# Latent attention, pair by pair: values summed one pair later, both heads' weights turned in a row, Silu behind the exponentials

## The chip, the cores and the metric

The kernel runs on one core of one Trainium2 chip. The metric is the device time of one execution in microseconds (us). TensorE (PE, with its weight loads as PEld), VectorE (DVE), ScalarE (ACT), GpSimd (POOL) and SyncE (SP) each work through their own list of instructions in order and wait for each other by semaphores that only count up.

## What is computed

Two blocks are applied to one sequence of 256 tokens of width 1024. The first is a retention layer (4 heads) followed by a latent attention layer (16 heads); the second is a recurrent and attention hybrid with a feed-forward part. The change touches only the latent attention, which is

```
q = (_rms_norm(q_lat, q_norm) @ w_uq)       # 16 heads, 128 plain + 64 rotary columns each
kv = (lat @ w_up)                           # 128 key columns and 128 value columns per head
sc = (q_nope . k_nope + rope(q) . k_rope) * scale     # causal, two blocks of 128 queries
p = softmax(sc)
o = p @ v
return (o * silu(gate)) @ w_out
```

## The kernel before

Every weight matrix comes from HBM in units of up to 128x2048 numbers, four raw slots deep (`load`, issued on SP). ACT rounds a unit to its high part (`act_hi`, L1039), DVE subtracts to get the low part (`dve_lo`, L1496), and PE multiplies in three terms, high x high, high x low, low x high (`mm3`, L364 to L366). `act_hi(u)` waits until PE has finished unit u-4 (semaphore `w_used`), `dve_lo(u)` waits for `act_hi(u)`, and PE waits for `dve_lo(u)` before unit u. Both splitting steps are written three units ahead of PE (`AHEAD`).

The 16 heads go in 8 pairs. Pair `pair` uses four units: gate, two of the query, one of keys and values. On PE these give four groups of projections, and the attention of the pair before is put between them: the scores (`pe_scores`, L674 and L679) after the gate unit; the turning of head 0's softmax weights (`pe_turn_p`, L689, three transposes of 128x128) after the query units; head 1's turning and both heads' values (`pe_values`, L699 and L700) after the key and value unit. The eighth pair's attention stands between the first units of the output projection (`pe_output`, unit 0 to 5, with "hooks" called ahead of a unit; `U_BOUT` is the number of its first unit).

Around that, DVE masks the scores (`dve_masked`, L1756), ACT takes the exponentials (`act_exps`, L1189), DVE divides by the sum (`dve_normal`, L1767 and L1770, which raises `b_p`), PE turns, ACT copies the turned weights to SBUF (`act_pT`, L1198, which raises `b_pT`), PE sums the values, DVE multiplies by the gate (`dve_og`, L1779), ACT rounds (`act_oT`, L1203), POOL makes the low part (`pool_oT`, L2136). ACT also takes Silu of the gate projection (L1213), and copies queries and keys (L1223, L1231); DVE copies the values' projection (`b_v`, L1809) and makes the rotary products (L1732, L1735). Silu and Exp lie in different tables, so ACT loads a table ahead of each.

The order on each engine is written out by hand. In the output projection DVE's list is `lo(U_BOUT+3)`, `lo(U_BOUT+4)`, masked head 0, masked head 1, normal head 0, `lo(U_BOUT+5)`, normal head 1, `lo(U_BOUT+6)` and so on: head 1's weights are divided behind the splitting of unit `U_BOUT+5`, whose `act_hi` waits until PE has finished unit `U_BOUT+1`.

Of the kernel before, what the change touches and what calls it, by code (L numbers as in the profile page):

```python
# [6 lines left out]
ACT = mybir.ActivationFunctionType  # L7
# [696 lines left out]
def pe_pair(k, pair):  # L704

    T, s, ps = k.T, k.s, k.ps
    u = U_PAIR + 4 * pair
    if pair:
        T.wait_ge(s["b_gate"], pair)
    feature_major(k, u, k.xT, KD, 2 * VH, halves(ps[:, 0, :]))  # L710
    if pair == 0:
        T.wait_ge(s["b_lat"], 1)
        for n in range(2):
            pe_turn_pair(k, "lat", n, lambda t, c: k.b_lat[:, t, c * P:(c + 1) * P], ps[:, 4 + n, :])
        T.wait_ge(s["turned_lo"], TURN["qlat"] + 3)
    else:
        pe_scores(k, pair - 1)
        T.wait_ge(s["b_qn"], pair)
    for n in range(2):
        wh, wl = weights(k, u + 1 + n, 3, 2 * QC)  # L720
        for q, out in enumerate((ps[:, 1, 0:S], ps[:, 1, S:2 * S], ps[:, 2, 0:S])):
            if q == 2 and n == 0 and pair:
                T.wait_ge(s["b_turned"], pair)
            for c in range(3):
                m = mm3(k, out, tuple(z[:, c, q * P:(q + 1) * P] for z in (wh, wl)),
                        tuple(z[:, 3 * n + c, :] for z in k.b_qlatT), n == 0 and c == 0 and q != 1, n == 1 and c == 2)
                if q == 0 and c == 0 and head_signals(u + 1 + n):
                    m.then_inc(s["w_head"], 1)
        m.then_inc(s["w_used"], 1)
    if pair:  # L730
        pe_turn_p(k, pair - 1, 0)
        T.wait_ge(s["b_kn"], pair)
    else:
        T.wait_ge(s["turned_lo"], TURN["lat"] + 2)
    wh, wl = weights(k, u + 3, 4, 2 * KC)
    for h in range(2):
        for c in range(4):
            m = mm3(k, ps[:, 3, h * S:(h + 1) * S], tuple(z[:, c, h * P:(h + 1) * P] for z in (wh, wl)),
                    tuple(z[:, c, :] for z in k.b_latT), h == 0 and c == 0, c == 3)
            if h == 0 and c == 0 and head_signals(u + 3):  # L740
                m.then_inc(s["w_head"], 1)
    if pair:
        T.wait_ge(s["b_v"], pair)
    for t in range(NT):
        for c in range(4):
            m = mm3(k, ps[:, 4, t * S:(t + 1) * S], tuple(z[:, c, t * P:(t + 1) * P] for z in k.b_latT),
                    tuple(z[:, c, 2 * NOPE:2 * KC] for z in (wh, wl)), t == 0 and c == 0, c == 3)
    m.then_inc(s["w_used"], 1)
    if pair:
        pe_turn_p(k, pair - 1, 1)  # L750
        pe_values(k, pair - 1, 0)
        pe_values(k, pair - 1, 1)


def pe_attention_hooks(k):
    T, s, last = k.T, k.s, HB // 2 - 1

    def banks_read():
        T.wait_ge(s["b_gate"], last + 1)
        T.wait_ge(s["b_qn"], last + 1)  # L760

    def outputs_split():
        T.wait_ge(s["b_oT_lo"], last)

    def keys_read():
        T.wait_ge(s["b_turned"], last + 1)
        T.wait_ge(s["b_kn"], last + 1)

    def last_split():
        T.wait_ge(s["b_oT_lo"], last + 1)  # L770

    return {0: [banks_read],
            1: [lambda: pe_scores(k, last)],
            2: [lambda: pe_turn_p(k, last, 0), outputs_split],
            3: [lambda: pe_values(k, last, 0), lambda: pe_turn_p(k, last, 1), keys_read],
            4: [lambda: pe_values(k, last, 1)],
            6: [last_split]}


# [421 lines left out]
def act_oT(k, pair):  # L1201
    k.A.wait_ge(k.s["b_og"], pair + 1)
    k.A.activation(k.b_oT[0][:, 2 * pair:2 * pair + 2, :], k.b_og[:, :, :], ACT.Copy).then_inc(k.s["b_oT_hi"], 1)  # L1203


def act_pair(k, pair):
    A, s, ps, par = k.A, k.s, k.ps, pair % 2
    u = U_PAIR + 4 * pair
    act_hi(k, u + AHEAD)
    A.wait_ge(s["w_used"], u + 1)  # L1210
    if pair >= 2:
        A.wait_ge(s["b_og"], pair - 1)
    A.activation(k.b_gate[:, par, :, :], ps[:, 0, :].rearrange("p (h s) -> p h s", h=2), ACT.Silu).then_inc(s["b_gate"], 1)  # L1213
    if pair:
        act_exps(k, pair - 1, 0)
        act_exps(k, pair - 1, 1)
    else:
        for n in range(2):
            act_turned(k, "lat", n, ps[:, 4 + n, :], k.b_latT[0], k.b_kvnorm)
    act_hi(k, u + 1 + AHEAD)  # L1220
    act_hi(k, u + 2 + AHEAD)
    A.wait_ge(s["w_used"], u + 3)
    A.activation(k.b_qn[:, par, :, :], ps[:, 1, :].rearrange("p (h s) -> p h s", h=2), ACT.Copy).then_inc(s["b_qn"], 1)  # L1223
    if pair:
        act_pT(k, pair - 1, 0)
    act_hi(k, u + 3 + AHEAD)
    if pair:
        act_pT(k, pair - 1, 1)
        act_oT(k, pair - 1)
    A.wait_ge(s["w_used"], u + 4)  # L1230
    A.activation(k.b_kn[:, par, :, :], ps[:, 3, :].rearrange("p (h s) -> p h s", h=2), ACT.Copy).then_inc(s["b_kn"], 1)  # L1231


def act_attention_output(k):

    A, s, d, last = k.A, k.s, k.d, HB // 2 - 1
    act_hi(k, U_BOUT + AHEAD)
    act_hi(k, U_BOUT + 1 + AHEAD)
    act_exps(k, last, 0)
    act_exps(k, last, 1)  # L1240
    act_hi(k, U_BOUT + 2 + AHEAD)
    act_pT(k, last, 0)
    act_hi(k, U_BOUT + 3 + AHEAD)
    act_pT(k, last, 1)
    act_hi(k, U_BOUT + 4 + AHEAD)
    act_oT(k, last)
    act_hi(k, U_BOUT + 5 + AHEAD)

    A.wait_ge(s["b_oT_lo"], last + 1)
    for n, name in enumerate(("ln_g", "ln_b")):  # L1250
        act_dma(k, "lnw1_in", k.lnw[1][:, n, :], d[name][1:2, :].broadcast_to([P, D]))
    act_dma(k, "columns_in", k.c_columns[:, :], d["columns"])
    act_dma(k, "kw_in", k.c_kw_raw[:, :, :].rearrange("p k n -> p (k n)"), d["w_ikw"])
    act_dma(k, "rgw_in", k.c_rgw[:, :, :, :].rearrange("p a k n -> p (a k n)"), d["rg_w"])
    act_hi(k, U_BOUT + 6 + AHEAD)
# [527 lines left out]
def dve_pair(k, pair):  # L1783
    V, s, ps, par = k.V, k.s, k.ps, pair % 2
    u = U_PAIR + 4 * pair
    dve_lo(k, u + AHEAD)
    if pair:
        dve_masked(k, pair - 1, 0)
        dve_masked(k, pair - 1, 1)
    else:  # L1790
        dve_key_rotary(k)
        for n in range(2):
            dve_turned(k, "lat", n, ps[:, 4 + n, :], k.b_latT, k.b_kvnorm)
    if pair:
        dve_normal(k, pair - 1, 0)
        dve_normal(k, pair - 1, 1)
    dve_lo(k, u + 1 + AHEAD)
    dve_lo(k, u + 2 + AHEAD)
    V.wait_ge(s["w_used"], u + 3)
    if pair:  # L1800
        V.wait_ge(s["b_qr"], pair)
    else:
        V.wait_ge(s["b_kr"], 1)
    dve_rotary(k, ps[:, 2, 0:S]).then_inc(s["b_turned"], 1)
    dve_lo(k, u + 3 + AHEAD)
    if pair:
        dve_og(k, pair - 1)
    V.wait_ge(s["w_used"], u + 4)
    V.tensor_copy(k.b_v[:, par, :, :], ps[:, 4, :].rearrange("p (t n) -> p t n", t=2)).then_inc(s["b_v"], 1)  # L1809


def dve_attention_output(k):
    last = HB // 2 - 1
    dve_lo(k, U_BOUT + AHEAD)
    dve_lo(k, U_BOUT + 1 + AHEAD)
    dve_masked(k, last, 0)
    dve_masked(k, last, 1)
    dve_normal(k, last, 0)
    dve_lo(k, U_BOUT + 2 + AHEAD)
    dve_normal(k, last, 1)  # L1820
    dve_lo(k, U_BOUT + 3 + AHEAD)
    dve_lo(k, U_BOUT + 4 + AHEAD)
    dve_og(k, last)
    dve_lo(k, U_BOUT + 5 + AHEAD)
    dve_lo(k, U_BOUT + 6 + AHEAD)
# [314 lines left out]
def pool_program(k):  # L2140
    G, s = k.G, k.s
    G.wait_ge(s["ropeA_in"], 16)
    sin = k.a_rope[:, 1:2, :].broadcast_to([P, 4, S])
    for h in range(HA):
        G.wait_ge(s["a_raw"], 2 * h + 2)
        if h:
            G.wait_ge(s["a_rope"], h)
        G.tensor_tensor(k.a_tsin[:, :, :], k.a_raw[:, :, :], sin, ALU.mult).then_inc(s["a_sin"], 1)
        G.wait_ge(s["a_gate"], h + 1)
        G.wait_ge(s["a_o"], h + 1)  # L2150
        G.tensor_tensor(k.a_o[:, 0, :], k.a_o[:, 0, :], k.a_g[:, 0, :], ALU.mult).then_inc(s["a_gated0"], 1)
    for pair in range(HB // 2):
        if pair:
            pool_oT(k, pair - 1)
        G.wait_ge(s["b_turned"], pair + 1)
        G.tensor_tensor(k.b_qr[:, pair % 2, :], k.b_xc[:, :], k.b_xs[:, :], ALU.add).then_inc(s["b_qr"], 1)
    pool_oT(k, HB // 2 - 1)
    pool_hybrid(k)


# [129 lines left out]
```

## Time and profile before

| | us |
|---|---|
| median of 3 runs | 884.99 (884.75 to 885.15) |
| the profiled execution | 885.22 |
| its span, first to last instruction | 883.9 |
| PE busy | 876.4 (99%) |
| DVE busy | 604.7 (68%) |
| ACT busy | 496.0 (56%) |
| POOL busy | 76.7 (9%) |

Busy time says which engine has no room; the start times of PE's instructions in a row say where PE lost time, since the end of a matmul in the profile is modelled. The eight pairs lie between about 240 and 413 us of the span, the output projection from there to about 460 us.

### The profile page before, as it was taken

How to read it: one execution, taken by the hardware profiler on the slowest of the kernel's cores; microseconds unless marked ns; L12 is line 12 of the kernel's file. 1: busy time of each engine (PE TensorE's matmuls, PEld its weight loads, DVE VectorE, ACT ScalarE, POOL GpSimd, SP SyncE). 2: the span in 40 equal slices, each digit the busy share in tenths (PEclk: the TensorE clock that was granted, in tenths of full speed). 3: DMA queues.
4: the chain of work that ended last, by engine and by line, in shares of the span. 5: the costliest groups of instructions: out<-in, count | busy, mean ns of one | idle time of the engine just before them, and what ended most of it. 6: DMA issues, size and time to landing. Idle time of an engine off the chain costs nothing.

```text
span 883.9 us, 13288 instructions
## 1 busy us (share of the span) xinstructions
PE 876.4 (99%) x5577; PEld 781.1 (88%) x5577; DVE 604.7 (68%) x827; ACT 496.0 (56%) x629; POOL 76.7 (9%) x50
## 2 busy tenths in 40 slices
PE   8999999999999999999999999999999999999998
PEld 7798888888999999999888899999999888888887
DVE  5866665649896666666468787778967755657441
ACT  6454444444666666666437667897753554455330
POOL 0110101000010000000000000224000012221000
PEclk9999999999999999999999999999999999999999
DMA  8835554642744444455564544324345644455720
GB/s 345 330 138 191 183 199 161 208 158 66 271 156 147 149 150 149 151 191 191 191 254 143 209 172 154 133 96 144 143 144 198 231 143 165 169 189 205 255 89 24
DMA packets 24684, 154.31 MB, mean 175 GB/s; under 512 B 3120, under 2 KB 3376, under 8 KB 8880
## 3 DMA queue, kind: packets, MB, share of 16 engines
q1 hardware_dynamic: 22880, 148.97, 46.8%
q10 hardware_dynamic: 1584, 3.96, 1.5%
q8 instruction: 44, 0.72, 0.3%
q0 software_dynamic: 160, 0.52, 0.1%
q14 instruction: 16, 0.13, 0.0%
HBM read 152.39 MB, written 1.05 MB: 174 GB/s over the span
## 4 chain that ended last, share of the span: by engine, by line
PE 85%; DVE 8%; ACT 4%; DMA 1%; issue 1%; SPq 0%; ACTq 0%; DVEq 0%
PE ps L364 23%; PE ps L365 23%; PE ps L366 23%; DVE w_lo_ring L1496 4%; ACT w_hi_ring L1039 3%; PE ps L447 2%; DMA w_raw<-in_a_w_in 1%; PE ps L674 1%; DVE c_fr L2117 1%; PE ps L699 1%; PE ps L463 1%; ACT c_p L1446 1%; PE ps L450 1%; DVE c_fr L2115 1%; PE ps L679 1%
## 5 line engine op out<-in xcount | busy, mean ns | idle before, releaser
L1496 DVE TENSOR_TENSOR w_lo_ring<-w_raw,w_hi_ring 128x2048 fp32r<-128x2048 f32 x146 | 333.8, 2299 | 176.9 <-ACT w_hi_ring L1039 176.4
L1039 ACT ACTIVATE w_hi_ring<-w_raw 128x2048 fp32r<-128x2048 f32 x146 | 277.9, 1914 | 111.4 <-PE ps L366 102.2
L364 PE MATMUL ps<-xT_hi,w_hi_ring 128*128 128x256 f32 x488 | 138.6, 284 | 0.0
L365 PE MATMUL ps<-xT_lo,w_hi_ring 128*128 128x256 f32 x488 | 136.7, 280 | 0.0
L366 PE MATMUL ps<-xT_hi,w_lo_ring 128*128 128x256 f32 x488 | 136.5, 280 | 0.0
L364 PE MATMUL ps<-w_hi_ring,xT_hi 128*128 128x512 f32 (+1 forms) x240 | 95.1, 396 | 0.5 <-DVE w_lo_ring L1496 0.5
L364 PEld LDWEIGHTS ps<-xT_hi,w_hi_ring 128*128 128x128 f32 x488 | 92.1, 189 | 1.9 <-issue 0.8
L366 PE MATMUL ps<-w_hi_ring,xT_lo 128*128 128x512 f32 (+1 forms) x240 | 92.8, 387 | 0.0
L365 PEld LDWEIGHTS ps<-xT_lo,w_hi_ring 128*128 128x128 f32 x488 | 92.1, 189 | 0.6
L365 PE MATMUL ps<-w_lo_ring,xT_hi 128*128 128x512 f32 (+1 forms) x240 | 92.6, 386 | 0.0
L366 PEld LDWEIGHTS ps<-xT_hi,w_lo_ring 128*128 128x128 f32 x488 | 92.1, 189 | 0.0
L447 PE MATMUL ps<-xw,w_hi_ring 128*128 128x512 f32 x240 | 75.4, 395 | 0.0
L450 PEld LDWEIGHTS ps<-xw,w_lo_ring 128*128 128x128 f32 x240 | 45.1, 188 | 10.7
L364 PEld LDWEIGHTS ps<-w_hi_ring,xT_hi 128*128 128x128 f32 x240 | 45.1, 188 | 9.6 <-issue 1.6
L365 PEld LDWEIGHTS ps<-w_lo_ring,xT_hi 128*128 128x128 f32 x240 | 45.1, 188 | 9.0 <-issue 1.0
L366 PEld LDWEIGHTS ps<-w_hi_ring,xT_lo 128*128 128x128 f32 x240 | 45.0, 188 | 9.0
L364 PE MATMUL ps<-w_hi_ring,c_fT_hi 128*128 128x512 f32 x128 | 49.9, 390 | 0.3 <-DVE w_lo_ring L1496 0.3
L365 PE MATMUL ps<-w_lo_ring,c_fT_hi 128*128 128x512 f32 x128 | 49.8, 389 | 0.0
L366 PE MATMUL ps<-w_hi_ring,c_fT_lo 128*128 128x512 f32 x128 | 49.8, 389 | 0.0
L450 PE MATMUL ps<-xw,w_lo_ring 128*128 128x256 f32 x240 | 47.1, 278 | 0.0
L364 PE MATMUL ps<-b_qlatT_hi,w_hi_ring 128*128 128x256 f32 x144 | 41.0, 285 | 0.0
L366 PE MATMUL ps<-b_qlatT_hi,w_lo_ring 128*128 128x256 f32 x144 | 40.2, 279 | 0.0
(334 smaller groups left out, 1738.4 us busy)
## 6 DMA issues: line engine op xcount, KB each, us to landing
w_raw<-in_a_w_in SPq DMA_DIRECT2D x22, 1024.0 KB, 5.0
w_raw<-in_w_ff_in SPq DMA_DIRECT2D x16, 1024.0 KB, 4.8
w_raw<-in_w_ff_out SPq DMA_DIRECT2D x16, 1024.0 KB, 5.0
w_raw<-in_b_w_uq SPq DMA_DIRECT2D x16, 576.0 KB, 4.6
w_raw<-in_a_w_out SPq DMA_DIRECT2D x8, 1024.0 KB, 4.8
w_raw<-in_b_w_gate SPq DMA_DIRECT2D x8, 1024.0 KB, 4.9
w_raw<-in_kv_w_up SPq DMA_DIRECT2D x8, 1024.0 KB, 4.8
w_raw<-in_b_w_out SPq DMA_DIRECT2D x8, 1024.0 KB, 4.9
```

Source lines behind the costliest of these rows:

```text
L364: k.T.matmul(out, lh, rh, start=start, stop=False, skip_group_check=True)
L365: k.T.matmul(out, lh, rl, start=False, stop=False, skip_group_check=True)
L366: return k.T.matmul(out, ll, rh, start=False, stop=stop, skip_group_check=True)
L447: k.T.matmul(out, wh[:, n, c * P:(c + 1) * P], xw[:, n, :, :].rearrange("p a s -> p (a s)"), start=n == 0, stop=False, skip_group_check=True)
L450: m = k.T.matmul(out[:, 0:S], wl[:, n, c * P:(c + 1) * P], xw[:, n, 0, :], start=False, stop=n == KD - 1, skip_group_check=True)
L463: m = k.T.transpose(bank[:, (2 * n + t) * P:(2 * n + t + 1) * P], src(t, 2 * pair + n), k.ident[:, :])
L674: T.matmul(ps[:, 5 + h, cols], k.b_qn[:, par, h, qs], k.b_kn[:, par, h, keys], start=qs.start == 0, stop=False, skip_group_check=True)
L679: m = T.matmul(ps[:, 5 + h, cols], k.b_qr[rows, par, qs], k.b_kr[rows, keys], start=False, stop=True, skip_group_check=True)
L699: T.matmul(out, k.b_v[:, par, 0, cols], k.b_pT[:, h, 0:2 * P], start=h == 0, stop=False, skip_group_check=True)
L1039: k.A.activation(k.hi[:, in_slot(u)], k.raw[u % RING][:, :], ACT.Copy).then_inc(k.s["w_hi"], 1)
L1446: m = A.activation(k.c_p[:, r, cols], k.c_p[:, r, cols], ACT.Exp, bias=k.c_smx[:, q, r:r + 1], scale=head_scale(k, g)[:, q, r:r + 1], accu ...
L1496: k.V.tensor_tensor(k.lo[:, in_slot(u)], k.raw[u % RING][:, :], k.hi[:, in_slot(u)].bitcast(F32), ALU.subtract).then_inc(k.s["w_lo"], 1)
```

## The change

On PE, the values of pair p are no longer summed at the end of iteration p+1 but in iteration p+2, right behind the scores of pair p+1; both heads' weights are turned in one place, between the query units and the key and value unit. In the output projection the seventh pair's values stand behind the eighth's scores (hook 1), both turnings at hook 2 and both values at hook 3. On ACT, Silu goes behind the exponentials and behind the rounding of the output two pairs back. On DVE, `dve_og` goes behind the masks, and on POOL `pool_oT` follows one pair later. In the output projection DVE's own order changes only by `dve_og(last - 1)`.

```diff
@@ pe_pair
     else:
         pe_scores(k, pair - 1)
+        if pair >= 2:
+            for h in range(2):
+                pe_values(k, pair - 2, h)
         T.wait_ge(s["b_qn"], pair)
...
     if pair:
         pe_turn_p(k, pair - 1, 0)
+        pe_turn_p(k, pair - 1, 1)
         T.wait_ge(s["b_kn"], pair)
...
     m.then_inc(s["w_used"], 1)
-    if pair:
-        pe_turn_p(k, pair - 1, 1)
-        pe_values(k, pair - 1, 0)
-        pe_values(k, pair - 1, 1)
@@ pe_attention_hooks
     def outputs_split():
-        T.wait_ge(s["b_oT_lo"], last)
+        T.wait_ge(s["b_oT_lo"], last - 1)
...
-            1: [lambda: pe_scores(k, last)],
-            2: [lambda: pe_turn_p(k, last, 0), outputs_split],
-            3: [lambda: pe_values(k, last, 0), lambda: pe_turn_p(k, last, 1), keys_read],
-            4: [lambda: pe_values(k, last, 1)],
+            1: [lambda: pe_scores(k, last), lambda: pe_values(k, last - 1, 0), lambda: pe_values(k, last - 1, 1)],
+            2: [lambda: pe_turn_p(k, last, 0), lambda: pe_turn_p(k, last, 1), outputs_split],
+            3: [lambda: pe_values(k, last, 0), lambda: pe_values(k, last, 1), keys_read],
             6: [last_split]}
@@ act_pair
     act_hi(k, u + AHEAD)
-    A.wait_ge(s["w_used"], u + 1)
-    if pair >= 2:
-        A.wait_ge(s["b_og"], pair - 1)
-    A.activation(k.b_gate[:, par, :, :], ps[:, 0, :].rearrange("p (h s) -> p h s", h=2), ACT.Silu).then_inc(s["b_gate"], 1)
     if pair:
         act_exps(k, pair - 1, 0)
         act_exps(k, pair - 1, 1)
-    else:
+    if pair >= 2:
+        act_oT(k, pair - 2)
+    A.wait_ge(s["w_used"], u + 1)
+    A.activation(k.b_gate[:, par, :, :], ps[:, 0, :].rearrange("p (h s) -> p h s", h=2), ACT.Silu).then_inc(s["b_gate"], 1)
...
     if pair:
         act_pT(k, pair - 1, 0)
+        act_pT(k, pair - 1, 1)
     act_hi(k, u + 3 + AHEAD)
-    if pair:
-        act_pT(k, pair - 1, 1)
-        act_oT(k, pair - 1)
@@ act_attention_output
     act_exps(k, last, 1)
+    act_oT(k, last - 1)
     act_hi(k, U_BOUT + 2 + AHEAD)
     act_pT(k, last, 0)
+    act_pT(k, last, 1)
     act_hi(k, U_BOUT + 3 + AHEAD)
-    act_pT(k, last, 1)
@@ dve_pair
         dve_masked(k, pair - 1, 1)
+        if pair >= 2:
+            dve_og(k, pair - 2)
...
     dve_lo(k, u + 3 + AHEAD)
-    if pair:
-        dve_og(k, pair - 1)
@@ dve_attention_output
     dve_masked(k, last, 1)
+    dve_og(k, last - 1)
     dve_normal(k, last, 0)
@@ pool_program
-        if pair:
-            pool_oT(k, pair - 1)
+        if pair >= 2:
+            pool_oT(k, pair - 2)
...
-    pool_oT(k, HB // 2 - 1)
+    for pair in (HB // 2 - 2, HB // 2 - 1):
+        pool_oT(k, pair)
```

How this moves the instructions is shown at three places. The first is PE at the end of the last pair, before; `b_p` are the softmax weights, `b_pT` the turned ones, `b_v` the values, and L364 in the last row is the output projection's first matmul.

```order
L366 MATMUL ps<-w_hi_ring,b_latT_lo 128x256
L689 MATMUL ps<-ident,b_p 128x128 x3
L699 MATMUL ps<-b_pT,b_v 128x256
L700 MATMUL ps<-b_pT,b_v 128x128
L699 MATMUL ps<-b_pT,b_v 128x256
L700 MATMUL ps<-b_pT,b_v 128x128
L364 MATMUL ps<-w_hi_ring,b_oT_hi 128x512
```

The values stood right behind the turning of head 1. After the change nothing stands there, and the values are behind the next scores (`b_kn`, `b_qn` and `b_kr`, `b_qr`), here those of hook 1:

```order
L366 MATMUL ps<-w_hi_ring,b_oT_lo 128x512
L674 MATMUL ps<-b_kn,b_qn 128x128
L674 MATMUL ps<-b_kn,b_qn 128x256
L674 MATMUL ps<-b_kn,b_qn 128x128
L674 MATMUL ps<-b_kn,b_qn 128x256
L679 MATMUL ps<-b_kr,b_qr 128x128 x2
L679 MATMUL ps<-b_kr,b_qr 128x256 x2
L699 MATMUL ps<-b_pT,b_v 128x256
L700 MATMUL ps<-b_pT,b_v 128x128
L699 MATMUL ps<-b_pT,b_v 128x256
```

These four value matmuls use weights turned a whole pair earlier. The second place is PE between units 1 and 2 of the output projection (hook 2), first before and then after; `b_oT` is the gated attention output.

```order
L366 MATMUL ps<-w_hi_ring,b_oT_lo 128x512
L689 MATMUL ps<-ident,b_p 128x128 x3
L364 MATMUL ps<-w_hi_ring,b_oT_hi 128x512
L365 MATMUL ps<-w_lo_ring,b_oT_hi 128x512
L366 MATMUL ps<-w_hi_ring,b_oT_lo 128x512
```

```order
L366 MATMUL ps<-w_hi_ring,b_oT_lo 128x512
L689 MATMUL ps<-ident,b_p 128x128 x6
L364 MATMUL ps<-w_hi_ring,b_oT_hi 128x512
L365 MATMUL ps<-w_lo_ring,b_oT_hi 128x512
L366 MATMUL ps<-w_hi_ring,b_oT_lo 128x512
```

Head 1's three transposes moved ahead of all of unit 2; DVE's division for head 1 did not move with them. The third place is ACT in one pair, before and then after (`b_gate` is Silu, `w_hi_ring` the `act_hi` of the units).

```order
L1213 ACTIVATE b_gate<-ps 128x512
L1189 ACT_TABLE_LOAD
L1189 ACTIVATE b_p,b_few<-b_p,b_few 128x128
L1189 ACTIVATE b_p,b_few<-b_p,b_few 128x256
L1189 ACTIVATE b_p,b_few<-b_p,b_few 128x128
L1189 ACTIVATE b_p,b_few<-b_p,b_few 128x256
L1039 ACTIVATE w_hi_ring<-w_raw_50 128x2048
L1039 ACTIVATE w_hi_ring<-w_raw_51 128x2048
L1223 ACTIVATE b_qn<-ps 128x512
```

```order
L1188 ACT_TABLE_LOAD
L1188 ACTIVATE b_p,b_few<-b_p,b_few 128x128
L1188 ACTIVATE b_p,b_few<-b_p,b_few 128x256
L1188 ACTIVATE b_p,b_few<-b_p,b_few 128x128
L1188 ACTIVATE b_p,b_few<-b_p,b_few 128x256
L1202 ACTIVATE b_oT_hi<-b_og 128x512
L1215 ACT_TABLE_LOAD
L1215 ACTIVATE b_gate<-ps 128x512
L1038 ACTIVATE w_hi_ring<-w_raw_50 128x2048
L1038 ACTIVATE w_hi_ring<-w_raw_51 128x2048
```

Rounding, table load and Silu now stand between the exponentials and the two `act_hi`.

## Rows read from the trace of the kernel before

**Rows 1.** The page, busy time, share and instructions of each engine.

```profile
PE 876.4 (99%) x5577; PEld 781.1 (88%) x5577; DVE 604.7 (68%) x827; ACT 496.0 (56%) x629; POOL 76.7 (9%) x50
```

**Rows 2.** Waits of PE over the span: us in total, times, longest.

```profile
PE ps L519 <- DVE a_warm L1543: 1.5, 1, 1.5
...
PE ps L858 <- DVE c_yaT_lo L2099: 0.3, 1, 0.3
```

**Rows 3.** Timeline, pair's end: start, us, engine, line, operation, [idle <-releaser].

```profile
300.90 0.49 PE L689 MATMUL ps<-ident,b_p 128*128 128x128 f32 x3
301.23 0.60 PE L699 MATMUL ps<-b_pT,b_v 128*128 128x256 f32 x2
301.43 0.49 ACT L1198 ACTIVATE b_pT<-ps 128x384 f32<-128x384 f32 x1 [3.51 <-PE ps L689]
301.66 0.38 PE L700 MATMUL ps<-b_pT,b_v 128*128 128x128 f32 x2
301.97 0.70 PE L699 MATMUL ps<-b_pT,b_v 128*128 128x256 f32 x2
...
302.51 0.38 PE L700 MATMUL ps<-b_pT,b_v 128*128 128x128 f32 x2
302.65 0.37 PE L364 MATMUL ps<-xT_hi,w_hi_ring 128*128 128x256 f32 x1
...
324.71 0.37 PE L364 MATMUL ps<-xT_hi,w_hi_ring 128*128 128x256 f32 x1
```

**Rows 4.** Timeline of PE at hook 3 of the output projection.

```profile
432.19 0.59 PE L699 MATMUL ps<-b_pT,b_v 128*128 128x256 f32 x2
432.62 0.38 PE L700 MATMUL ps<-b_pT,b_v 128*128 128x128 f32 x2
432.84 0.49 PE L689 MATMUL ps<-ident,b_p 128*128 128x128 f32 x3
```

**Rows 5.** Line 1198: what ended its idle time, us in total, times.

```profile
  PE ps L689: 24.5, 7
```

**Rows 6.** Timeline of PEld at the ends of the rotary part of one scores group.

```profile
287.67 0.52 PEld L679 LDWEIGHTS ps<-b_kr,b_qr 64*128 64x128 f32 x8 [0.33 <-issue]
...
288.52 0.19 PEld L364 LDWEIGHTS ps<-b_qlatT_hi,w_hi_ring 128*128 128x128 f32 x1 [0.33 <-issue]
```

**Rows 7.** Timeline of ACT and DVE in the same pair.

```profile
286.47 0.60 ACT L1213 ACTIVATE b_gate<-ps 128x512 f32<-128x512 f32 x1 [0.66 <-PE ps L366]
...
287.08 1.28 ACT L1189 ACT_TABLE_LOAD   x1
...
291.29 3.70 ACT L1039 ACTIVATE w_hi_ring<-w_raw 128x2048 fp32r<-128x2048 f32 x2
...
293.22 4.49 DVE L1496 TENSOR_TENSOR w_lo_ring<-w_raw,w_hi_ring 128x2048 fp32r<-128x2048 f32 x2 [1.05 <-ACT w_hi_ring L1039]
...
303.54 0.68 DVE L1809 COPY b_v<-ps 128x512 f32<-128x512 f32 x1
```

**Rows 8.** Timeline around hook 2 of the output projection.

```profile
425.04 0.55 DVE L1770 TENSOR_SCALAR b_p<-b_p,b_few 128x128 f32<-128x128 f32 x2
...
426.38 0.49 PE L689 MATMUL ps<-ident,b_p 128*128 128x128 f32 x3
426.64 1.92 ACT L1039 ACTIVATE w_hi_ring<-w_raw 128x2048 fp32r<-128x2048 f32 x1 [0.95 <-PE ps L366]
...
428.59 2.29 DVE L1496 TENSOR_TENSOR w_lo_ring<-w_raw,w_hi_ring 128x2048 fp32r<-128x2048 f32 x1 [3.00 <-ACT w_hi_ring L1039]
...
430.99 0.55 DVE L1770 TENSOR_SCALAR b_p<-b_p,b_few 128x128 f32<-128x128 f32 x2
```

**Rows 9.** Windows: stretch, its length, PE busy (x instructions), granted clock, DMA share, GB/s.

```profile
412.00:450.00 38.00, 38.00 (x181) 1.00 0.56 194
```

**Rows 10.** First matmuls of the span: durations ns min/median/max; the same merged.

```profile
L519 PE MATMUL ps<-a_warm x13: 387/628/794, 1.5 to 5.8; 128*128 128x512 f32 x13
...
1.46 4.78 PE L519 MATMUL ps<-a_warm 128*128 128x512 f32 x13 [1.46 <-DVE a_warm L1543]
```

More of the change, by code:

```diff
@@ L1216, in act_pair @@
         act_exps(k, pair - 1, 1)
-    else:
+    if pair >= 2:
+        act_oT(k, pair - 2)
+    A.wait_ge(s["w_used"], u + 1)
+    A.activation(k.b_gate[:, par, :, :], ps[:, 0, :].rearrange("p (h s) -> p h s", h=2), ACT.Silu).then_inc(s["b_gate"], 1)
+    if pair == 0:
         for n in range(2):
```

## The prediction

> **What bounds the kernel now.** I read the page's busy times first: PE is busy 99% of the span, DVE 68%, ACT 56% [rows 1]. Then PE's own waits: the longest in the whole span is the 1.5 us for its first operand [rows 2]. So there is no long stall to remove, and every stall that is added lands on the end in full unless PE waits later for something that has caught up meanwhile. Since the ends of matmuls are modelled, short stalls don't show as idle time; they show as a start that comes later than the same sequence starts elsewhere. So the third view is the timeline, read by start times, at the places that the change touches.
>
> One pair lasts 324.71 - 302.65 = 22.06 us on PE [rows 3]. At its end PE turns head 1's weights, sums head 0's values, and then needs head 1's turned weights, which ACT is still copying: the copy runs from 301.43 to 301.92, and head 1's values start at 301.97. Unhindered, values of a head take 0.43 us to L700 and 0.22 us more to what follows: 432.19, 432.62, 432.84 [rows 4]. Here it is 0.43, then 301.97 - 301.66 = 0.31, then 302.51 - 301.97 = 0.54 [rows 3]. The stall is 0.09 + 0.11 = 0.20 us, the second part because a pipeline that ran empty starts late. ACT waited for this turning 7 times, once in each pair from the second to the eighth [rows 5]. Nothing else in a pair's PE list shows such a step: 150 projection matmuls and the attention's own fill it.
>
> **The change, part by part.** No matmul, transpose, copy or table load is added or removed. Only places change, so the sum is over stalls.
>
> 1. Values behind the next scores. Their turned weights were copied a pair earlier, their bank 7 was read by `dve_og` a pair earlier, their values are in the other half of a doubled buffer. No wait stands there, and the 0.20 us goes 7 times: -1.4 us. Behind a stall something may be late next: the scores now hold up the query units by the values' 1.3 us, but that is the same work moved within the pair.
>
> 2. Scores to values on PE. The rotary part uses 64 rows; entering it and leaving it each show 0.33 us of weight loading idle on "issue" [rows 6]. Leaving it now goes to value matmuls instead of projections, both of 128 rows. The trace of before doesn't show this neighbour. At best one such gap is hidden, 7 x 0.33 = 2.3 us saved; at worst one more comes, 2.3 us lost. I take zero, because the other changes between kinds of matmul, from projections to transposes and from values to projections, cost nothing beyond the pieces themselves: three transposes take 0.33 us to the next start [rows 3].
>
> 3. Both turnings in a row, within the pairs. Head 1's weights must be ready at the end of the query units. DVE's divisions follow the exponentials, which end where the two `act_hi` begin, 291.29 [rows 7]. A division takes some 0.2 + 0.55 us [rows 8], and `dve_og`, a pass over 128x512 like the `b_v` copy's 0.68 [rows 7], now goes ahead of them: both are ready by about 293. Before, the turning of head 0 was followed by the 48 matmuls of the key and value unit, each at most 22.06 / 150 = 0.147 us, and by 302.65 - 300.90 = 1.75 us at the end [rows 3]; so it began at 293.8 at the earliest, and now 1.3 us later, at 295.1. Cost nothing; at least 2 us of cover.
>
> 4. Silu behind the exponentials. ACT now has rounding (0.6 us, a pass over 128x512 like Silu), table load 1.28 and Silu 0.60 [rows 7] ahead of the two `act_hi`: they start about 2.5 us later, at 293.8 instead of 291.29. DVE's two low parts follow, 295.7 to 300.2. The first of them belongs to the next pair's gate unit and ends at about 298.0, and PE starts that unit at 302.65: 4.5 us of cover are left. Further down DVE's list, `b_v` ends at about 305.3 instead of 304.22 (DVE's list is 2.5 us later, but the wait for the values and the 0.7 of `dve_og` ahead of the copy are gone); the next scores need it about when Silu could start, 286.47 + 22.06 = 308.5. Cost nothing, 3 us of cover left. If that cover were gone, each us would be paid in each of 7 pairs.
> The raw slots are then also freed 2.5 us later, so SP issues the loads later; each has a whole pair, 22 us, until its `act_hi`. POOL's rotary sum no longer stands behind the rounding of the same pair and comes earlier. Nothing.
>
> 5. Both turnings in a row at hook 2. Here the new wait is. DVE's order there is masks, `dve_og`, normal head 0, low part of unit `U_BOUT+5`, normal head 1. The low part waits for ACT's high part, and that for PE's end of unit 1, which is exactly where hook 2 stands. Before, PE turned head 0 there, streamed unit 2, and turned head 1 behind it. The rows are the chain: PE arrives at 426.38, the high part runs from 426.64 (0.26 behind, the drain of the last matmul) to 428.56, the low part from 428.59 to 430.88, the division ends at 430.99 + 0.55 = 431.54 [rows 8]. So head 1's weights exist 5.16 us after PE arrives, whatever the absolute time is, since every step hangs on PE's arrival. Head 0's were ready at 425.59, 0.8 us ahead [rows 8]; the chain to them hangs on the end of unit 0, behind which 0.7 us of `dve_og` now comes on DVE and 1.3 us of values on PE, so 1.4 us of cover are left. PE issues its three transposes, 0.33 us, and stands until 5.16 plus 0.05 for the semaphore (the step from 301.92 to 301.97 in [rows 3]) and 0.1 for the empty pipeline: 5.3 - 0.33 = 5.0 us. Queued behind it are head 1's transposes and all of units 2 to 7. Bounds: 4.8 us without the two small terms; 5.3 if the first transposes hide nothing. I take 5.0.
>
> Is it paid back? The longest of PE's waits behind the pairs is 0.3 us [rows 2], so there is no later wait to swallow it. Hooks 3 to 6 have no stall to lose: values start where the stream reaches them [rows 4].
>
> Sum: 885.22 - 1.4 + 5.0 = 888.8 us for the profiled execution (its span 883.9 + 3.6 = 887.5, with 1.3 around it). The median of the runs is 0.23 below the profiled execution: 884.99 + 3.6 = 888.6 us.
>
> **Rivals.**
>
> *The clock falls in the gap.* PE would stand still for 5 us in mid-kernel, which it never does now; the granted clock of the stretch reads 1.00, the 2.4 GHz level [rows 9]. How slow matmuls look is seen at the start of the span, after idling: 13 matmuls of 512 columns with a median of 628 ns against a least of 387, over 4.78 us [rows 10], although the clock column says nothing of it. At the pace of the output projection, (432.19 - 426.38 - 0.33) / 24 = 0.228 us each, they would take 12 x 0.228 + 0.39 = 3.1 us. The start lost 1.7 us to the 1.2 GHz level. The same after the gap gives 888.6 + 1.7 = 890.3. A longer slow stretch, of all of unit 2, would lose 5.5 us at the most. For it: a fully idle gap of 5 us. Against it: nothing in this trace shows a fall after a gap, since there is none.
> The Trainium skill, TensorE: Matmul & The Clock Gate, section "HAM oscillation — how this bites in real kernels", says that an idle gap that is long enough halves the array's clock, and that it must be earned back by steady work; by that page this rival would hold wherever 5 us are long enough. The trace agrees on the start of the span and shows nothing of a gap.
>
> *Merging saves more than the stall: not slower.* If the weight loading's idle time at both ends of the rotary part, 2 x 0.33 us, vanished in 7 groups because value matmuls are queued behind, 4.6 us would go beside the 1.4, and 5.0 would come: 884.0. It decides from 0.5 us per pair on. Against it: entering the rotary part isn't touched at all, and leaving it meets the same 128-row kind as before. With one end alone it is 886.3.
>
> *ACT or DVE becomes late in the pairs.* If the cover of 3 us in step 4 were used up and 0.5 us too much, 7 pairs would lose 3.5 us: 892.1. Against it: ACT's 3.51 us of idle ahead of head 1's copy [rows 3] lies in the same pair and takes up the shift.
>
> *The hook's wait isn't there.* DVE would have to divide head 1 ahead of the low part. Its order says otherwise; the kernel would then take 884.99 - 1.4 = 883.6.
>
> **How the numbers follow.** Forecast 888.6, chance 0.56, its own range 888.0 to 889.4. Clock 0.33, 890.3, reaching to 892. Not slower by merging 0.04, with one end alone 0.02. Late in the pairs 0.03. No wait 0.02. The range of 887.6 to 891.4 holds the forecast, most of the clock's case and an error of 0.1 us per pair on either side. A difference of 0.2%, 1.8 us, is about what can be told from no change here. Faster by more: 0.03. Within: 0.04. Slower by more: 0.93.
>
> **What would show it.** Right: the first copy of `b_pT` no longer waits in the middle of values, and a pair lasts 21.86 us instead of 22.06 (22.1 or more if step 4 fails, 21.5 if merging saves); a gap of about 4.9 us on PE with DVE's `b_p` as releaser, at about 425 to 430 us; unit 2 behind it with starts 0.23 us apart, or 0.45 if the clock fell, with the granted clock below 1.00 there. Wrong: no gap at hook 2, or a wait of the scores for `b_v`, or of the gate unit for its low part.

## The result, and the profile after

The changed kernel takes 890.53 us (median of 6 runs, 890.23 to 891.26) against 885.2 us (884.75 to 885.43) before: the ratio is 1.0062 with a 95% interval of 1.0051 to 1.0073. It is slower by 5.3 us. The profiled execution took 890.85 us, its span 889.5 instead of 883.9: 5.6 us more. The forecast was slower by 3.6 us, 888.6, with 888.0 to 889.4 as its own range. The time lies outside that, in the wider range of 887.6 to 891.4, at the place of the rival in which the clock falls (890.3).

The list of PE's waits now begins with a wait that no row before had [rows 2]; columns as there.

```profile
PE ps L689 <- DVE b_p L1768: 4.7, 1, 4.7
PE ps L519 <- DVE a_warm L1541: 1.5, 1, 1.5
PE ps L364 <- DVE w_lo_ring L1494: 1.1, 2, 0.7
```

The lines of DVE and ACT have moved by one or two: L1768 is the division that was L1770. The timeline around hook 2 answers to [rows 8]:

```profile
424.94 0.49 PE L689 MATMUL ps<-ident,b_p 128*128 128x128 f32 x3
425.20 1.91 ACT L1038 ACTIVATE w_hi_ring<-w_raw 128x2048 fp32r<-128x2048 f32 x1 [1.70 <-PE ps L366]
...
427.14 2.29 DVE L1494 TENSOR_TENSOR w_lo_ring<-w_raw,w_hi_ring 128x2048 fp32r<-128x2048 f32 x1 [3.98 <-ACT w_hi_ring L1038]
...
429.55 0.55 DVE L1768 TENSOR_SCALAR b_p<-b_p,b_few 128x128 f32<-128x128 f32 x2
...
430.15 0.90 PE L689 MATMUL ps<-ident,b_p 128*128 128x128 f32 x3 [4.72 <-DVE b_p L1768]
430.71 0.78 PE L364 MATMUL ps<-w_hi_ring,b_oT_hi 128*128 128x512 f32 x1
...
431.28 0.63 PE L365 MATMUL ps<-w_lo_ring,b_oT_hi 128*128 128x512 f32 x1
431.71 0.63 PE L366 MATMUL ps<-w_hi_ring,b_oT_lo 128*128 128x512 f32 x1
...
438.25 0.59 PE L699 MATMUL ps<-b_pT,b_v 128*128 128x256 f32 x2
```

PE arrives at 424.94, turns head 0, and stands until 430.15. Every link of the chain has the length that it had before, to 0.01 us: high part 0.26 us behind PE's arrival, low part at 427.14, division done at 430.10, 5.16 us behind the arrival. Without the wait, head 1's transposes would have begun at 424.94 + 0.33 = 425.27, so the wait costs 4.88 us. Then look at the starts behind it: 431.28 to 431.71 is 0.43 us for a matmul of 512 columns, where the output projection had 0.228. The windows tell why (stretch, length, PE busy, granted clock, DMA share, GB/s):

```profile
426.00:428.00 2.00, 0.00 (x0) 1.00 0.00 0
428.00:430.00 2.00, 0.00 (x0) 0.54 0.00 0
430.00:432.00 2.00, 1.85 (x6) 0.50 0.71 188
432.00:434.00 2.00, 2.00 (x6) 0.50 0.80 336
434.00:436.00 2.00, 2.00 (x9) 0.76 0.00 0
436.00:438.00 2.00, 2.00 (x10) 1.00 0.00 0
```

The granted clock went from 1.00 to 0.50, the 1.2 GHz level, while PE stood idle. It came back to 1.00, the 2.4 GHz level, at about 435.0, when PE had worked for almost 5 us. From 430.15 to the values at 438.25 it took 8.10 us; the same work takes 5.86 us at the high level (the run with the filled gap, below). The clock costs 2.24 us in this trace.

In the pairs the gain is there. The timeline of PE in two successive pairs, the scores and the values now behind them:

```profile
306.52 1.47 PE L674 MATMUL ps<-b_kn,b_qn 128*128 128x128 f32 x8
307.92 0.93 PE L679 MATMUL ps<-b_kr,b_qr 64*128 64x128 f32 x8
308.78 0.70 PE L699 MATMUL ps<-b_pT,b_v 128*128 128x256 f32 x2
309.31 0.38 PE L700 MATMUL ps<-b_pT,b_v 128*128 128x128 f32 x2
309.54 0.60 PE L699 MATMUL ps<-b_pT,b_v 128*128 128x256 f32 x2
309.97 0.38 PE L700 MATMUL ps<-b_pT,b_v 128*128 128x128 f32 x2
...
328.40 1.47 PE L674 MATMUL ps<-b_kn,b_qn 128*128 128x128 f32 x8
```

From scores to scores it is 21.88 us instead of 22.06 [rows 3]. Head 1's values follow L700 by 0.23 us, where [rows 4] have 0.22 and [rows 3] 0.31. Over seven pairs that is 1.3 us. The sum from the trace: hook 2 is reached 1.44 us earlier (424.94 for 426.38; 0.1 us of it was there at the first scores already, 264.1 for 264.2), the wait adds 4.88, the clock 2.24, together 5.7 us; the spans differ by 5.6.

ACT and DVE in one pair, which answers to [rows 7]:

```profile
291.60 0.60 ACT L1215 ACTIVATE b_gate<-ps 128x512 f32<-128x512 f32 x1
292.09 3.71 ACT L1038 ACTIVATE w_hi_ring<-w_raw 128x2048 fp32r<-128x2048 f32 x2
```

```profile
302.95 0.69 DVE L1807 COPY b_v<-ps 128x512 f32<-128x512 f32 x1
```

Silu stands directly ahead of the two high parts. The copy of `b_v` ends at 303.64, and the scores at 306.52 are not held up: 2.9 us of cover are left. The weight loading's idle time at the end of the rotary part has moved from L364 [rows 6] to L699. For L699, what ended its idle time, us in total and times:

```profile
  issue: 2.3, 7
```

That is again 0.33 us each, once for each pair whose values stand behind scores. L364 has 4.3 us in 13 times where it had 6.3 in 20.

### The profile page after: what moved, and what is told of

The parts are those of the page before. It is cut to its first block, busy times and chain, and to the rows that moved or that the text cites. A ratio compares the mean times of both kernels' runs of the same rounds, so it can differ in the third digit from the quotient of the medians.

```text
span 889.5 us, 13284 instructions
## 1 busy us (share of the span) xinstructions
PE 877.4 (99%) x5577; PEld 782.3 (88%) x5577; DVE 603.0 (68%) x827; ACT 496.9 (56%) x631; POOL 92.2 (10%) x50
## 4 chain that ended last, share of the span: by engine, by line
PE 84%; DVE 8%; ACT 5%; DMA 1%; issue 1%; SPq 0%; ACTq 0%; DVEq 0%
PE ps L364 23%; PE ps L366 23%; PE ps L365 23%; DVE w_lo_ring L1494 4%; ACT w_hi_ring L1038 3%; PE ps L447 2%; DMA w_raw<-in_a_w_in 1%; PE ps L674 1%; DVE c_fr L2116 1%; PE ps L699 1%; PE ps L463 1%; ACT c_p L1444 1%; PE ps L450 1%; DVE c_fr L2114 1%; PE ps L679 1%
## 5 line engine op out<-in xcount | busy, mean ns | idle before, releaser
L364 PE MATMUL ps<-xT_hi,w_hi_ring 128*128 128x256 f32 x488 | 138.1, 283 | 0.0
L364 PE MATMUL ps<-w_hi_ring,xT_hi 128*128 128x512 f32 (+1 forms) x240 | 95.1, 396 | 0.7 <-DVE w_lo_ring L1494 0.7
L364 PEld LDWEIGHTS ps<-xT_hi,w_hi_ring 128*128 128x128 f32 x488 | 92.1, 189 | 1.9 <-issue 0.8
L364 PEld LDWEIGHTS ps<-w_hi_ring,xT_hi 128*128 128x128 f32 x240 | 45.1, 188 | 9.9 <-issue 1.9
L364 PE MATMUL ps<-w_hi_ring,c_fT_hi 128*128 128x512 f32 x128 | 49.9, 390 | 0.3 <-DVE w_lo_ring L1494 0.3
L364 PE MATMUL ps<-b_qlatT_hi,w_hi_ring 128*128 128x256 f32 x144 | 40.9, 284 | 0.0
```

Of the source, the lines that this page charges most:

```text
L364: k.T.matmul(out, lh, rh, start=start, stop=False, skip_group_check=True)
```

## The experiments

The kernel before was timed again beside each of them, and each ratio is to that time.

**The division ahead of the low part.** The changed kernel, with one swap in `dve_attention_output`:

```diff
     dve_normal(k, last, 0)
-    dve_lo(k, U_BOUT + 2 + AHEAD)
     dve_normal(k, last, 1)
+    dve_lo(k, U_BOUT + 2 + AHEAD)
```

> The changed kernel, with DVE dividing head 1's weights ahead of the low part of unit U_BOUT+5. My theory (the changed kernel loses only by the wait at hook 2 and the low clock behind it, and gains 0.2 us in each of 7 pairs): 885.2 - 1.4 = 883.8 us, no gap at hook 2, clock 1.00 throughout. Rival (the order in the pairs gains nothing, or Silu's new place costs): 885.2 or more. Rival (merging saves more): below 883.

883.88 us (883.25 to 884.31) against 885.32, ratio 0.9984 (0.9975 to 0.9993). The mean granted clock was 1.00. Measured from the kernel before, it is 6.8 us below the changed kernel (-1.4 against +5.3). Its timeline at hook 2:

```profile
423.67 0.55 DVE L1768 TENSOR_SCALAR b_p<-b_p,b_few 128x128 f32<-128x128 f32 x2
...
425.34 0.82 PE L689 MATMUL ps<-ident,b_p 128*128 128x128 f32 x6
425.60 1.92 ACT L1038 ACTIVATE w_hi_ring<-w_raw 128x2048 fp32r<-128x2048 f32 x1 [1.71 <-PE ps L366]
```

The division ends 1.1 us before PE comes, and six transposes go in a row. So all of the loss hangs on this one place in DVE's list, and the rest of the change gains 1.4 us, as expected. This version beats both kernels.

**The same swap in the kernel before.**

> The kernel before with the same swap on DVE. There PE turns head 1 only behind unit 2, so nothing waits for the division: 885.2 us, unchanged within 0.3. Rival (the swap itself gains, by giving DVE a better order): below 884.9, and then the gain of e1 would not be the change's.

885.12 us (884.89 to 885.98) against 885.32, ratio 1.0 (0.9991 to 1.0009). The swap gains nothing by itself; the gain of the run above is the change's own.

**Turned in a row alone.** The kernel before with, in the pairs, only this:

```diff
         pe_turn_p(k, pair - 1, 0)
+        pe_turn_p(k, pair - 1, 1)
         T.wait_ge(s["b_kn"], pair)
...
-        pe_turn_p(k, pair - 1, 1)
         pe_values(k, pair - 1, 0)
...
         act_pT(k, pair - 1, 0)
+        act_pT(k, pair - 1, 1)
     act_hi(k, u + 3 + AHEAD)
     if pair:
-        act_pT(k, pair - 1, 1)
         act_oT(k, pair - 1)
```

> The kernel before, in which in the pairs only the turning of head 1 moves next to that of head 0 (on PE and ACT); values stay at the end of the same iteration, the output projection is as before. If the gain is only the stall between the two heads' values: 883.8 us, a pair of 21.87 us. Rival (the values need to come a pair later for it): 885.2.

883.92 us (883.67 to 884.13), ratio 0.9985 (0.9976 to 0.9994). The values at a pair's end, to be read against [rows 3]:

```profile
301.13 0.59 PE L699 MATMUL ps<-b_pT,b_v 128*128 128x256 f32 x2
301.56 0.38 PE L700 MATMUL ps<-b_pT,b_v 128*128 128x128 f32 x2
301.78 0.60 PE L699 MATMUL ps<-b_pT,b_v 128*128 128x256 f32 x2
302.21 0.38 PE L700 MATMUL ps<-b_pT,b_v 128*128 128x128 f32 x2
```

0.22 us from L700 to the other head, 0.43 us more to the next L700: both halves of the stall are gone. Summing the values a pair later, in the run with the division ahead (883.88), adds nothing to that. The whole gain of the change is in one of its three parts.

**Silu alone.** The kernel before with the exponentials ahead of Silu in `act_pair`:

```diff
     act_hi(k, u + AHEAD)
+    if pair:
+        act_exps(k, pair - 1, 0)
+        act_exps(k, pair - 1, 1)
     A.wait_ge(s["w_used"], u + 1)
...
-    if pair:
-        act_exps(k, pair - 1, 0)
-        act_exps(k, pair - 1, 1)
-    else:
+    if pair == 0:
```

> The kernel before, in which only Silu moves behind the exponentials on ACT. Covered by slack: 885.2 us within 0.3, with the two high parts behind it some 1.9 us later in each pair. Rival (a late high part reaches PE): at least 0.2 us in each of 7 pairs, 886.6 or more.

885.25 us (884.87 to 885.6), ratio 1.0 (0.9991 to 1.0009). What the delay used up shows in what ended the idle time of line 1198, of which [rows 5] had 24.5 us:

```profile
  PE ps L689: 13.0, 7
```

That is (24.5 - 13.0) / 7 = 1.6 us of ACT's slack per pair, where 1.9 was expected, and the kernel is no slower.

**The output projection's hooks alone.** The kernel before with

```diff
-            2: [lambda: pe_turn_p(k, last, 0), outputs_split],
-            3: [lambda: pe_values(k, last, 0), lambda: pe_turn_p(k, last, 1), keys_read],
-            4: [lambda: pe_values(k, last, 1)],
+            2: [lambda: pe_turn_p(k, last, 0), lambda: pe_turn_p(k, last, 1), outputs_split],
+            3: [lambda: pe_values(k, last, 0), lambda: pe_values(k, last, 1), keys_read],
```

and ACT's two copies in a row there.

> The kernel before, in which only the hooks of the output projection change: both turnings at hook 2, both values at hook 3. If wait and clock are all that the output projection adds: 885.2 + 4.9 + 2.4 = 892.5 us; without a fall of the clock 890.1. Rival (the wait arises only with the new order of the pairs): 885.2.

892.06 us (891.13 to 892.42) against 885.03, ratio 1.0077 (1.0064 to 1.0089): 7.0 us by the medians, where wait and clock of the changed kernel's trace make 4.88 + 2.24 = 7.1. The wait is the same, and stands in the timeline between these two turnings:

```profile
PE ps L689 <- DVE b_p L1769: 4.7, 1, 4.7
...
426.08 0.49 PE L689 MATMUL ps<-ident,b_p 128*128 128x128 f32 x3
431.29 0.90 PE L689 MATMUL ps<-ident,b_p 128*128 128x128 f32 x3 [4.72 <-DVE b_p L1769]
```

The clock fell here too, but later in the gap:

```profile
429.00:429.50 0.50, 0.00 (x0) 1.00 0.00 0
429.50:430.00 0.50, 0.00 (x0) 0.70 0.00 0
430.00:431.00 1.00, 0.00 (x0) 0.50 0.00 0
```

PE's last transpose ended at 426.57, so it had been idle for about 3 us while the granted clock still read 1.00. From the second turning to the values it took 8.30 us (431.29 to 439.59), 2.44 more than at the high level.

**The gap filled.** To part the clock from the wait, PE was kept at work while it waited (the changed kernel, with this between the two turnings at hook 2):

```diff
+    def fill():
+        T.wait_ge(s["b_og"], last)
+        for _ in range(5):
+            T.matmul(k.ps[:, 7, :], k.b_kn[:, last % 2, 0, 0:P], k.b_kn[:, last % 2, :, :].rearrange("p h s -> p (h s)"),
+                     start=True, stop=True, skip_group_check=True)
```

> The changed kernel, in which PE multiplies keys by keys five times (128x512, f32, about 0.88 us each by the scores' rows, 4.4 us together) into a bank that is free, between the two turnings at hook 2; their result is overwritten. PE still waits for the same division, but is idle for under 0.7 us. If the clock costs 2.4 us of the changed kernel's loss: the clock stays at 1.00 and the time is 883.8 + 4.9 = 888.7 us. Rival (the slow matmuls behind the gap have another cause, such as late operands): 890.5 as the changed kernel.

889.01 us (888.47 to 889.18) against 885.03, ratio 1.0043 (1.0029 to 1.0057). PE's timeline:

```profile
425.67 4.46 PE L765 MATMUL ps<-b_kn 128*128 128x512 f32 x10
...
430.56 0.55 PE L689 MATMUL ps<-ident,b_p 128*128 128x128 f32 x3 [0.43 <-DVE b_p L1774]
...
431.18 0.39 PE L365 MATMUL ps<-w_lo_ring,b_oT_hi 128*128 128x512 f32 x1
431.40 0.39 PE L366 MATMUL ps<-w_hi_ring,b_oT_lo 128*128 128x512 f32 x1
...
436.42 0.59 PE L699 MATMUL ps<-b_pT,b_v 128*128 128x256 f32 x2
```

The wait for the division is as long, 5.2 us from arrival, and the clock stayed: 0.22 us from one matmul to the next, and 436.42 - 430.56 = 5.86 us to the values. So the slow matmuls came from the idling, not from late operands. Useless work of 4.5 us made the kernel faster by 1.35 us by the medians (5.33 over before becomes 3.98). From arrival to the values the traces differ by the full 2.24 us (13.31 against 11.07); but this execution came to hook 2 0.4 us later than the changed kernel's, a lag that it had at the first scores already (264.5 for 264.1), so of the 2.24 the spans show 1.7 (889.5 against 887.8).

**A shorter gap.** The changed kernel with

```diff
     dve_normal(k, last, 0)
-    dve_lo(k, U_BOUT + 2 + AHEAD)
+    k.V.wait_ge(k.s["w_hi"], U_BOUT + 2 + AHEAD + 1 - FIRST)
     dve_normal(k, last, 1)
+    dve_lo(k, U_BOUT + 2 + AHEAD)
```

> The changed kernel, with DVE dividing head 1's weights when the high part of unit U_BOUT+5 is there, ahead of the low part: the gap of PE at hook 2 is 0.26 + 1.92 + 0.75 + 0.05 - 0.33 = 2.7 us instead of 4.9. If the clock falls only in a gap as long as the changed kernel's: 883.8 + 2.7 = 886.5 us, clock 1.00. If it falls in this one too: a slow stretch behind it as in the changed kernel, 2.4 us more, 888.9.

888.19 us (887.86 to 888.59), ratio 1.0036 (1.0023 to 1.0048). The expectation was 886.5 with the clock up and 888.9 with a slow stretch as long as in the changed kernel. The gap is 2.5 us, and the clock fell all the same, but the slow stretch was shorter. The timeline at the second turning and at the values behind unit 2, and the windows:

```profile
428.40 0.90 PE L689 MATMUL ps<-ident,b_p 128*128 128x128 f32 x3 [2.52 <-DVE b_p L1768]
...
435.85 0.59 PE L699 MATMUL ps<-b_pT,b_v 128*128 128x256 f32 x2
```

```profile
428.00:430.00 2.00, 1.60 (x6) 0.60 0.00 0
430.00:432.00 2.00, 2.00 (x7) 0.55 0.51 66
432.00:434.00 2.00, 2.00 (x10) 1.00 0.78 328
```

In half microseconds the clock reads 0.89 from 428.00 to 428.50 and 0.50 behind it, so it fell only at the very end of the gap, at about 428.4. By the starts it was back at about 431.8, when PE had worked for 3.4 us. To the values it took 7.45 us (428.40 to 435.85) against 5.86: the clock cost 1.6 us, not the 2.4 that the expectation carried over.

**The same with one matmul in it.** One of the multiplications above ahead of the second turning, with the same arrival of the division:

> The kernel of e4 (head 1 divided when the high part is there; the idle gap was 2.5 us) with one multiplication of keys by keys (128x512, f32, 0.86 us by the filled gap's trace) ahead of the second turning; its result is overwritten. PE is then idle for about 1.7 us and arrives at the same time. If the slow clock comes only with gaps above this: 1.00 throughout and 883.9 + 2.7 = 886.6 us, 1.6 below e4's 888.2. If this gap is enough too: 888.2.

886.41 us (886.26 to 886.95) against 885.14, ratio 1.0014 (1.0005 to 1.0023). The gap and the windows:

```profile
428.35 0.55 PE L689 MATMUL ps<-ident,b_p 128*128 128x128 f32 x3 [1.66 <-DVE b_p L1773]
```

```profile
426.00:428.00 2.00, 0.69 (x2) 1.00 0.00 0
428.00:430.00 2.00, 1.65 (x9) 1.00 0.00 0
```

With 1.66 us idle the clock stayed; with 2.52 us it fell. The one matmul is worth 1.9 us by the medians (3.16 over before becomes 1.27), 1.6 of it between arrival at hook 2 and the values.

## Why the prediction was right, and where its size was off

The direction, the place, the wait and its cause held. That the clock stays at 2.4 GHz, as the forecast assumed, did not: the time came out as that of a rival with a chance of 0.33. Step by step:

1. The stall between the heads' values: forecast -1.4 us, measured -1.4 (the division ahead: 883.88 against 885.32; turning alone: 883.92). That this needs only step 3's turning and not the values a pair later, the prediction did not say; it put the gain under step 1.
2. Scores to values at zero: right. The 0.33 us idle on issue moved from L364 to L699, and a pair got shorter by 0.18 us, not by more or less. The rival in which merging saves more is out.
3. and 4. The cover: forecast 3 us for `b_v`, measured 2.9, and Silu alone costs nothing. The match is partly luck. The forecast had the copy end at 305.3 and the scores at 308.5; they came at 303.64 and 306.52. It had left out that the gate unit no longer stands behind 1.75 us of turning and values (302.65 - 300.90 in [rows 3]), which brings scores, exponentials and high parts forward (292.09 instead of the 293.8 forecast). Both ends of the cover moved by about as much.
5. The wait: forecast 5.0 us, measured 4.88, and the chain of 5.16 us was the same to the hundredth, since each link hangs on PE's arrival. The 0.05 for the semaphore came (430.10 to 430.15), the 0.1 for an empty pipeline did not.

The size was off by the clock. The forecast set it at zero with a chance of 0.56 and gave the rival 0.33 with 1.7 us; it fell in the profiled execution of all three kernels with a gap of 2.5 us or more, and cost 2.24 us here. So the term of the sum that was mis-sized is the clock, 0 put and 2.24 measured. The reason given for zero was that nothing in the trace shows a fall after a gap; but that trace has no such gap, so it said nothing for zero either. The 1.7 us were too small because the slow stretch was longer than the one that was priced: 4.85 us of work from 430.15 to about 435.0, at 0.43 us a matmul where 0.228 is the pace, loses an estimated 4.85 x (1 - 0.228 / 0.43) = 2.3 us. That the rival's 890.3 is so near to 890.5 is partly luck, a wait 0.1 us too long beside a clock 0.5 us too cheap.

The Trainium skill, TensorE: Matmul & The Clock Gate, section "HAM oscillation — how this bites in real kernels", on which that rival leaned, says that idling between matmuls throttles the clock again. The changed kernel's trace agrees: the granted clock fell to 0.50 in the gap and came back once PE was at work again.

What is left open is on what the fall depends. The idle time alone doesn't settle it: in the shorter gap the clock fell about 2.5 us after PE's last transpose, with the hooks alone only after about 3 us. Nor is the slow stretch the same in each run. The mean granted clock of the changed kernel was 0.996 in four runs and 0.998 in two, and of the hooks alone 0.996 in three (892.06 to 892.42 us) and 0.998 in two (891.13 and 891.24); in the shorter gap it was 0.998 in all five. So the low stretch was shorter in some runs than in the one whose trace is shown, and 2.24 us is its cost in that one.

## What to carry to other kernels

When work is moved up on one engine, look at what makes its operand and at what stands ahead of the maker in its own list: here a transpose moved ahead of unit 2, its division stayed behind a low part that hangs on the end of unit 1, and the chain back to the mover, with the clock that falls in the wait, is the whole price. Where TensorE is the bound and a wait of some microseconds can't be avoided, count the clock behind it too. Matmuls whose result is thrown away kept it up here, five of them in a wait of 4.9 us and one in a wait of 2.5 us. And try the parts of a change alone: one of the three gave all of the gain.

## What the runs showed of the hardware that was not expected

The clock fell in a gap of only 2.52 us and cost 1.6 us there (428.40 to the values at 435.85, 7.45 us against 5.86), while with 1.66 us it didn't. It can also read 1.00 for about 3 us of idling first, as with the hooks alone. A matmul that is worth nothing, 0.86 us of keys by keys, saved 1.9 us. The granted clock column reads 1.00 at the start of the span too, where matmuls of 512 columns are as slow (628 ns [rows 10]) as at 0.50 in mid-kernel (0.63 us); so the column alone doesn't show a slow start, and the durations have to be read beside it.
